# A mixture of experts in blocks of 32 tokens on four column quarters of TensorE, instead of blocks of 64 on two halves

## The chip, the cores and the metric

The kernel runs on one core of one Trainium2 chip. The metric is the device time of one execution in microseconds; lower is better. Median before: 3705.31 us over three runs (3697.03 to 3705.87).

## The reference, cut to what matters

Two transformer blocks over 512 positions of width 1024. The first has a token mixer and then a mixture of experts; the second has attention branches and gates. Only the mixture is touched:

```python
logits = h @ w_router + b_router              # 512 tokens, 32 experts
top_val, top_idx = lax.top_k(logits, 4)
gates = softmax(top_val)
# for each chosen (token, expert) pair:
u = xb @ w1[e] + b1[e]                        # 1024 -> 2048
glu = minimum(u[:, 0::2], 7.0)
lin = clip(u[:, 1::2], -7.0, 7.0)
act = glu * sigmoid(1.702 * glu) * (lin + 1.0)
y = act @ w2[e] + b2[e]                       # 1024 -> 1024
out[token] += gate * y
```

All data are fp32. There are 2048 pairs, and the weights of the 32 experts are 32 x 12 MB.

## The kernel before, in words

`program` runs a sequence of stages, one after the other, with a barrier between them. Three matter here.

`settle` (L1386) ends with the routing. VectorE takes the four best of each token and a rank of each pair within its expert. It counts the blocks of each expert by comparing its token count with `edges`, multiples of 64 (L1553 to L1556); `nblki` holds the counts, `first` the first block of each. L1568 to L1575 build two tables, `who` (token number at its place in a block) and `where` (block of each pair), and 16 matmuls (L1477) make of them `list`, the tokens of each block. `edges`, `halves` and `eye32` are constant tables. SP starts the first 9 weight pieces (EARLY) in this stage. `combine` (L1805), after the experts, gathers the written rows and weighs them.

`experts` (L1593) is the stage in between. Its weights come in pieces of 1 MB, 12 for an expert: eight of the first layer, four of the second. `piece_source` (L1583) says what a piece is: two row groups of 128 and 1024 columns. They lie in a ring of 20 places, `raw`. SP waits for the semaphore `used` in `reload`, piece by piece, and starts the transfer of the piece that is 20 further (L1621). An expert's pieces are released in its last block, since every block of the expert needs them.

Work runs in blocks of up to 64 tokens of one expert. Each engine has its own loop over experts and, inside, over the blocks of the expert, whose number it reads from `nblki` at run time. TensorE's order in one block is written out by hand: bias of the first column half (`bias(0)`, L1685, which picks the expert's bias with the table `pick`), pieces 0 to 3, bias of the second, pieces 4 to 6, the turning of the first activations (`turn_act(0)`, L1704), piece 7, pieces 8 and 9, `turn_act(1)`, the turning of the gathered rows of the next block (`turn_rows`, L1672 and L1674), pieces 10 and 11. A piece is four matmuls (L1698), 128 rows by 64 tokens against 512 columns: for each of two row groups one on each half of the array's columns, so that two run side by side. The two banks `WIDE` hold the first layer, `OUT` the second.

The other engines serve this. VectorE clips the two parts of the first layer (L1791, L1792), multiplies (L1795) and multiplies with ScalarE's sigmoid (L1798). ScalarE makes the sigmoid (L1759), copies the turned activations (L1765) and the turned rows (L1748), copies the result out of `OUT` (L1774) and starts two writes of it to `rows_out` (L1744). POOL makes the index of the next block's tokens (L1649), starts the gather of its rows (L1643) and makes `pick` (L1652). The semaphores between them count blocks (or two per block).

One other place is of use for the prediction: `rwkv_output` computes a part of the modulation at L1149 with four column quarters, 128 rows by 32 columns against 512 columns each.

Of the kernel before, what the change touches and what calls it, by code (L numbers as in the profile page):

```python
# [11 lines left out]
F32 = mybir.dt.float32  # L12
# [7 lines left out]
P = 128  # L20
# [13 lines left out]
E = 32  # L34
# [23 lines left out]
MAXB = 64  # L58

def constants():
# [11 lines left out]
        "edges": np.broadcast_to(64.0 * np.arange(1, 9)[None, :], (P, 8)),  # L73
        "token": P * np.arange(TT)[None, :] + p,
        "headrow": (p % 32) == np.arange(8)[None, :],
        "halves": (p // 64) == (f // 64),
# [1309 lines left out]
def settle(nc, A, ps, T, R, M, N, spill, rows_in, raw_in, stored, kmt):  # L1386
# [6 lines left out]
    with stage(nc, "b_in", "var_ready", "root_ready", "scaled", "normed", "taken", "h_ready", "kept", "saved", "turned", "ht_out", "high", "pool_step",  # L1393
# [6 lines left out]
        def _(sp):  # L1400
            sp.dma_start(R["wr"][:, :, :], A["w_router"][0].rearrange("(k p) e -> p k e", p=P)).then_inc(in_, 16)
            sp.dma_start(R["br"][:, :], A["b_router"]).then_inc(in_, 16)
            b1 = A["b1"][0].rearrange("e (p h n) -> h e p n", p=2, h=2)
            for i in range(4):
                sp.dma_start(N["b1r"][E * i:E * i + E, :].rearrange("e (p n) -> e p n", p=2), b1[i // 2]).then_inc(b_in, 16)
# [8 lines left out]
        def _(pool):  # L1414
# [9 lines left out]
            for i in (1, 3):  # L1424
                lo = slice(E * i, E * i + E)
                done(pool.tensor_tensor(M["b12"][lo, :], N["b1r"][lo, :], M["b12"][lo, :].bitcast(F32), ALU.subtract))

        @block.tensor
        def _(pe):
# [46 lines left out]
            for j in range(JK):  # L1476
                last = pe.matmul(ps[0:64, 7, 0:MAXB], R["who"][:, j, :], R["where"][:, j, :], start=(j == 0), stop=(j == JK - 1))  # L1477
# [3 lines left out]
        def _(act):  # L1481
# [17 lines left out]
            act.activation(M["b12"][:, :], N["b1r"][:, :], ACT.Copy).then_inc(high, 1)  # L1499
# [10 lines left out]
        def _(dve):  # L1510
# [55 lines left out]
            done(dve.scalar_tensor_tensor(out=R["row"][:, :], in0=R["blk"][:, :], scalar=64.0, in1=R["rank"][:, :], op0=ALU.mult, op1=ALU.add))  # L1566
            done(dve.tensor_copy(T["slot"][:, :], R["row"][:, :]))
            done(dve.tensor_tensor(R["over"][:, 0:JK, :], bc(R["rank"][:, :], 2, 8), bc(S("edges"), 1, JK), ALU.is_ge))  # L1568
            done(dve.tensor_reduce(R["low"][:, :], R["over"][:, 0:JK, :], AX_X, ALU.add))
            done(dve.tensor_tensor(R["blk"][:, :], R["blk"][:, :], R["low"][:, :], ALU.add))  # L1570
            done(dve.scalar_tensor_tensor(out=R["low"][:, :], in0=R["low"][:, :], scalar=-64.0, in1=R["rank"][:, :], op0=ALU.mult, op1=ALU.add))
            done(dve.tensor_tensor(R["who"][:, :, :], bc(S("iota")[:, 0:64], 1, JK), bc(R["low"][:, :], 2, 64), ALU.is_equal))
            who = R["who"][:, :, :].rearrange("p (t k) s -> p t (k s)", k=TOPK)
            done(dve.tensor_tensor(who, who, bc(S("token"), 2, TOPK * 64), ALU.mult))
            dve.tensor_tensor(R["where"][:, :, :], bc(S("iota")[:, 0:MAXB], 1, JK), bc(R["blk"][:, :], 2, MAXB), ALU.is_equal).then_inc(listed, 1)  # L1575
            dve.wait_ge(list_prod, 1)
            done(dve.tensor_copy(R["list"][:, :], ps[0:64, 7, 0:MAXB]))

def piece_source(A, e, s):  # L1580

    w1 = A["w1"][0, e].rearrange("(k p) n -> p k n", p=P)
    w2 = A["w2"][0, e].rearrange("(k p) n -> p k n", p=P)  # L1583
    if s < 8:
        return w1[:, 2 * (s % 4):2 * (s % 4) + 2, (s // 4) * D:(s // 4 + 1) * D]
    return w2[:, 2 * (s - 8):2 * (s - 8) + 2, :]

def experts(nc, A, ps, T, R, M, raw_in, stored, cleared, gathered, rows_in, rows_out):
# [3 lines left out]
    HT = 64  # L1593
    TURNED, ROWS_T = 5, 3
    WIDE = (0, 1)
    OUT = 2
    with stage(nc, "used", "indexed", "picked", "bias_done", "turned", "x_out", "biased", "mixed", "sig", "acted", "at", "at_out",
               "y_out", "written") as (
            block, used, indexed, picked, bias_done, turned, x_out, biased, mixed, sig, acted, at, at_out, y_out, written):

        def counter(eng, name, first=0):

            r = eng.alloc_register(name)
            eng.reg_mov(r, first)
            return r, lambda top=MAXB - 1: eng.snap(r, min_val=first, max_val=top)
# [55 lines left out]
        def _(pe):  # L1661
# [1398 lines left out]
```

## Time and profile before

| | |
|---|---|
| median of three runs | 3705.31 us |
| span of the profiled execution | 3706.0 us (no separate time of it is given; its span stands for it) |
| PE busy | 3295.0 us, 89% |
| PE weight loads | 2108.3 us, 57% |
| DVE, ACT, POOL busy | 1399.2, 984.3, 154.3 us |
| DMA | 647.39 MB, mean 175 GB/s |
| stretch of the experts, 979 to 2151 us | PE busy 1144.2 of 1172 us, clock 1.00, DMA share 0.93, 357 GB/s |
| stretch before it, 0 to 979 us | PE busy 780.3 us, DMA share 0.34 |
| stretch after it, 2151 to 3706 us | PE busy 1370.6 us, DMA share 0.26 |

### The profile page before, as it was taken

The numbers are of one execution on the slowest core, as the hardware profiler recorded it, in microseconds if no ns is written. First come the engines' busy times: TensorE is split into PE (matmuls) and PEld (weight loads), VectorE is DVE, ScalarE is ACT, GpSimd is POOL, SyncE is SP. The second block draws the span as 40 slices with busy tenths as digits, with TensorE's granted clock in tenths as the row PEclk, the third lists the DMA queues.
The fourth block names the chain that finished last, engine by engine and source line by source line (L and its number), as shares of the span: only waits on it lengthen the run. The fifth ranks groups of instructions, "written<-read, shape, count | busy, mean of one in ns | idle before, by whom it ended". The sixth has DMA issues, their size and how long they took to land. (4 is left out here: it accounts for less than half of the span.)

```text
span 3706.0 us, 63217 instructions
## 1 busy us (share of the span) xinstructions
PE 3295.0 (89%) x25517; PEld 2108.3 (57%) x25518; DVE 1399.2 (38%) x2384; ACT 984.3 (27%) x1766; POOL 154.3 (4%) x221
## 2 busy tenths in 40 slices
PE   3998788787799997999999969987899899878998
PEld 2878677676433332333333327865578778655787
DVE  5535545546211111111111146544643365446433
ACT  2333313312111111111111103343532233435321
POOL 0000000000300000000000010000000000000000
PEclk8999889888799999999999989997999999979999
DMA  6621320324789999998986944331033133310331
GB/s 217 237 97 33 98 94 8 98 71 157 298 297 396 366 400 399 396 397 320 397 312 244 385 172 122 99 49 35 1 93 101 45 115 101 47 35 1 94 100 57
DMA packets 273124, 647.39 MB, mean 175 GB/s; under 512 B 36890, under 2 KB 97050, under 8 KB 270978
## 3 DMA queue, kind: packets, MB, share of 16 engines
q1 hardware_dynamic: 251314, 605.12, 45.6%
q0 software_dynamic: 6224, 21.24, 1.8%
q10 hardware_dynamic: 15360, 17.82, 1.5%
q8 instruction: 167, 2.74, 0.3%
q14 instruction: 59, 0.48, 0.0%
HBM read 600.85 MB, written 43.27 MB: 174 GB/s over the span
## 5 line engine op out<-in xcount | busy, mean ns | idle before, releaser
L1698 PE MATMUL ps<-raw,ex_xT 128*64 128x512 f32 x3072 | 698.0, 599 | 21.8 <-DMA raw<-in_w_dram 21.7
L1698 PEld LDWEIGHTS ps<-raw,ex_xT 128*64 128x64 f32 x3072 | 206.6, 137 | 419.2 <-issue 375.9
L1791 DVE TENSOR_SCALAR ex_gl<-ps 128x256 f32<-128x256 f32 x96 | 40.8, 425 | 1014.4 <-PE ps L1698 1014.4
L1698 PE MATMUL ps<-raw,ex_aT 128*64 128x512 f32 x1536 | 350.8, 596 | 6.1 <-DMA raw<-in_w_dram 5.5
L1698 PEld LDWEIGHTS ps<-raw,ex_aT 128*64 128x64 f32 x1536 | 105.3, 137 | 205.0 <-issue 187.5
L1950 PE MATMUL ps<-zhi,hh 128*128 128x512 f32 (+1 forms) x448 | 169.8, 379 | 0.4 <-DVE hl L2080 0.4
L1951 PE MATMUL ps<-zlo,hh 128*128 128x512 f32 (+1 forms) x448 | 169.0, 377 | 0.0
L1952 PE MATMUL ps<-zhi,hl 128*128 128x512 f32 (+1 forms) x448 | 168.6, 376 | 0.0
L2497 PE MATMUL ps<-uu_hi,hh 128*128 128x512 f32 x384 | 151.9, 395 | 12.2 <-DVE uu_lo L2609 12.2
L2499 PE MATMUL ps<-uu_hi,hl 128*128 128x512 f32 x384 | 152.2, 396 | 0.0
L2498 PE MATMUL ps<-uu_lo,hh 128*128 128x512 f32 x384 | 152.0, 396 | 0.0
L2609 DVE TENSOR_TENSOR uu_lo<-u_raw,uu_hi 128x2048 fp32r<-128x2048 f32 x30 | 68.6, 2292 | 202.7 <-ACT uu_hi L2575 202.7
L1765 ACT ACTIVATE ex_aT<-ps 128x256 f32<-128x256 f32 x96 | 36.8, 383 | 406.4 <-PE ps L1704 406.4
L2497 PE MATMUL ps<-uu_hi,u_oh 128*128 128x512 f32 x320 | 126.7, 396 | 0.4 <-DVE u_ol L2614 0.4
L2071 DVE TENSOR_TENSOR zlo<-oT,zhi 128x1024 fp32r<-128x1024 f32 (+1 forms) x64 | 74.6, 1166 | 137.2 <-ACT zhi L1987 136.5
L2498 PE MATMUL ps<-uu_lo,u_oh 128*128 128x512 f32 x320 | 126.3, 395 | 0.0
L2499 PE MATMUL ps<-uu_hi,u_ol 128*128 128x512 f32 x320 | 126.3, 395 | 0.0
L1987 ACT ACTIVATE zhi<-oT 128x1024 fp32r<-128x1024 f32 (+1 forms) x64 | 64.9, 1014 | 215.5 <-PE ps L1952 155.6
L1759 ACT ACTIVATE ex_arow<-ex_gl 128x256 f32<-128x256 f32 x96 | 40.0, 417 | 300.1 <-DVE ex_gl L1791 300.1
L2575 ACT ACTIVATE uu_hi<-u_raw 128x2048 fp32r<-128x2048 f32 x30 | 57.3, 1915 | 213.2 <-PE ps L2499 207.2
L2307 ACT ACTIVATE za<-ps,nsa_nm 128x256 f32<-128x256 f32 (+3 forms) x160 | 81.1, 511 | 109.0 <-DVE nsa_nm L2331 109.0
L2270 PE MATMUL ps<-small,za 128*128 128x128 f32 x544 | 86.1, 291 | 16.2 <-DVE za L2342 16.2
(558 smaller groups left out, 6018.8 us busy)
## 6 DMA issues: line engine op xcount, KB each, us to landing
raw<-in_w_dram SPq DMA_DIRECT2D x384, 1024.0 KB, 19.3
oT<-in_w_in_dram SPq DMA_DIRECT2D x64, 512.0 KB, 3.6
u_raw<-in_w_in_dram SPq DMA_DIRECT2D x24, 1024.0 KB, 5.2
expert_out<-xn SPq DMA_DIRECT2D x4, 4096.0 KB, 16.8
expert_out<-ex_yrow ACTq DMA_DIRECT2D x98, 128.0 KB, 6.4
late_ada<-in_w_ada_dram SPq DMA_DIRECT2D x12, 1024.0 KB
early_w<-in_w_in_dram SPq DMA_DIRECT2D x10, 1024.0 KB, 6.6
mT<-in_w_ada_dram SPq DMA_DIRECT2D x4, 2048.0 KB, 19.9
```

The costliest lines, as they stand in the source:

```text
L1698: mm = pe.matmul(o, x, M["raw"][:, (slot + LATE_SLOTS) % RING, k, h * 512:(h + 1) * 512], start=(s >= 8 and kk == 0), stop=(kk == 7))
L1950: pe.matmul(o, x_hi, w_hi, start=(kk == 0), stop=False)
L1951: pe.matmul(o, x_hi, w_lo, start=False, stop=False)
L1952: last = pe.matmul(o, x_lo, w_hi, start=False, stop=(kk == KD - 1))
L1987: act.activation(hi[q % nh][cut], raw[q % nr][cut], ACT.Copy).then_inc(hi_done, 1)
L2071: dve.tensor_tensor(lo[q % nh][cut], raw[q % nr][cut], hi[q % nh][cut].bitcast(F32), ALU.subtract).then_inc(lo_done, 1)
L2270: mm = pe.transpose(ps[:, 4 + x, b * P:(b + 1) * P], Z["p"][:, i % NB, x, b * P:(b + 1) * P], S("ident"))
L2307: act.activation(Z["p"][:, i % NB, x, 0:u["n"]], ps[:, (i % 2) * 2 + x, 0:u["n"]], ACT.Exp, bias=Z["nm"][:, i % 4, x:x + 1], accum_out=Z[" ...
L2497: pe.matmul(o, x_hi, w_hi, start=first, stop=False)
L2498: pe.matmul(o, x_hi, w_lo, start=False, stop=False)
L2499: return pe.matmul(o, x_lo, w_hi, start=False, stop=last)
L2609: dve.tensor_tensor(lo[q % nh], raw[q % nr], hi[q % nh].bitcast(F32), ALU.subtract).then_inc(lo_done, 1)
```

## The change

Blocks hold 32 tokens (HT) and every expert has at least two of them, so each of its first and later blocks can be written out in the code. One matmul is 128 rows by 32 tokens against 512 columns, on a quarter of the array's columns; four stand side by side. In the first layer the quarters are the four column groups of the 2048, so it needs one bank in place of two, and the bias is one pair of matmuls over the whole bank (a high and a low part). In the second layer they are two halves of the 1024 rows of the sum by two column groups; the halves are added afterwards. A piece of the first layer is now one row group with all 2048 columns; a piece of the second is one row group of each half.

TensorE's order per block w: bias and first layer of w, turning of the activations of w-1, turning of the rows of w+1, second layer of w-1. Places of the first layer are released by `used1` in the expert's last block, those of the second by `used2`, in the first block of the next expert. ScalarE copies the upper half of the result (64 partitions), VectorE adds it to the lower, ScalarE starts the writes. ScalarE's loop body begins with the copy of the turned activations, then the turned rows, the sigmoid of the next block and the result.

For the given inputs the experts get these numbers of tokens (counted from the reference): 44, 173, 113, 53, 8, 58, 162, 39, 48, 26, 50, 21, 51, 17, 79, 21, 70, 52, 73, 42, 159, 35, 36, 87, 96, 69, 135, 57, 66, 55, 46, 7. In blocks of 64 that makes 1 or 2 or 3 blocks each, 48 in all; in blocks of 32, with at least two, 87: 2, 6, 4, 2, 2, 2, 6, then seven of 2, then 3, 2, 3, 2, 3, 2, 5, 2, 2, 3, 3, 3, 5, 2, 3, 2, 2, 2.

The diff, cut to its core:

```diff
-MAXB = 64
+MAXB = 128
+HT = 32
+EDGES = SEQ // HT
...
-                last = pe.matmul(ps[0:64, 7, 0:MAXB], R["who"][:, j, :], R["where"][:, j, :], start=(j == 0), stop=(j == JK - 1))
+                last = pe.matmul(ps[0:HT, 7, 0:MAXB], R["who"][:, j, :], R["where"][:, j, :], start=(j == 0), stop=(j == JK - 1))
...
-            done(dve.tensor_tensor(R["over"][:, :, :], bc(cnt, 2, 8), bc(S("edges"), 1, E), ALU.is_gt))
+            done(dve.tensor_tensor(R["over"][:, :, :], bc(cnt, 2, EDGES), bc(S("edges"), 1, E), ALU.is_gt))
             done(dve.tensor_reduce(R["nblk"][:, :], R["over"][:, :, :], AX_X, ALU.add))
+            done(dve.tensor_scalar(R["nblk"][:, :], R["nblk"][:, :], 1.0, None, ALU.max))
+            done(dve.tensor_copy(R["nblki"][:, 0, :], R["nblk"][:, :]))
             done(dve.tensor_scalar(R["nblk"][:, :], R["nblk"][:, :], 1.0, None, ALU.add))
-            done(dve.tensor_copy(R["nblki"][:, :], R["nblk"][:, :]))
+            done(dve.tensor_copy(R["nblki"][:, 1, :], R["nblk"][:, :]))
             done(dve.tensor_tensor_scan(R["first"][:, :], S("ones")[:, 0:E], R["nblk"][:, :], 0.0, ALU.mult, ALU.add))
...
 def piece_source(A, e, s):
 
-    w1 = A["w1"][0, e].rearrange("(k p) n -> p k n", p=P)
-    w2 = A["w2"][0, e].rearrange("(k p) n -> p k n", p=P)
     if s < 8:
-        return w1[:, 2 * (s % 4):2 * (s % 4) + 2, (s // 4) * D:(s // 4 + 1) * D]
-    return w2[:, 2 * (s - 8):2 * (s - 8) + 2, :]
+        return A["w1"][0, e].rearrange("(k p) (a n) -> p k a n", p=P, a=2)[:, s, :, :]
+    return A["w2"][0, e].rearrange("(h k p) n -> p k h n", p=P, h=2)[:, s - 8, :, :]
 
 
...
+                    if s < W1P:
+                        sp.wait_ge(used1, w * W1P + s + 1)
+                    else:
+                        sp.wait_ge(used2, w * W2P + s - W1P + 1)
+                    sp.dma_start(M["raw"][:, place(slot), :, :], piece_source(A, e + ahead // NP, ahead % NP)).then_inc(raw_in[slot], 16)
...
+            def bias(w):
+                pe.wait_ge(picked, w + 1)
+                pe.matmul(ps[:, WIDE, :], M["pick"][:, :], M["b12"][:, 0, :], start=True, stop=False)
+                pe.matmul(ps[:, WIDE, :], M["pick"][:, :], M["b12"][:, 1, :], start=False, stop=False).then_inc(bias_done, 1)
+            def landed(i, place_in_turns):
+                pe.wait_ge(raw_in[place_in_turns % NS], i * (16 * EU * NP // NS) + (16 * (place_in_turns // NS) + 16))
+            def first_layer(w, i, g, fresh):
+                pe.wait_ge(x_out, w + 1)
+                for s in range(W1P):
+                    if fresh:
+                        landed(i, g + s)
+                    for j in range(4):
+                        mm = pe.matmul(ps[HT * j:HT * j + HT, WIDE, :], M["xT"][:, s, :], M["raw"][:, place((g + s) % NS), j // 2, (j % 2) * 512:(j % 2) * 512 + 512],
+                                       start=False, stop=(s == W1P - 1))
+                    mm.then_inc(used1, 1)
+            def turn_act(w):
+                pe.wait_ge(acted, w + 1)
+                for i2 in range(2):
+                    mm = pe.transpose(ps[:, ROWS_T, i2 * P:(i2 + 1) * P], M["arow"][:, i2 * P:(i2 + 1) * P], S("ident"))
+                mm.then_inc(at, 1)
+            def second_layer(w, i, g, fresh):
+                pe.wait_ge(y_out, w + 1)
+                pe.wait_ge(at_out, w + 1)
+                for s in range(W2P):
+                    if fresh:
+                        landed(i, g + W1P + s)
+                    for half in range(2):
+                        for n in range(2):
+                            o = ps[HT * (2 * half + n):HT * (2 * half + n) + HT, OUT, :]
+                            mm = pe.matmul(o, M["aT"][:, 4 * half + s, :], M["raw"][:, place((g + W1P + s) % NS), half, n * 512:(n + 1) * 512],
+                                           start=(s == 0), stop=(s == W2P - 1))
+                    mm.then_inc(used2, 1)
+            def one_block(i, g, before, fresh):
+                w = now()
+                pe.wait_ge(emptied, w)
+                bias(w)
+                first_layer(w, i, g, fresh)
+                turn_act(w - 1)
+                turn_rows(w + 1)
+                second_layer(w - 1, i, before, before == g)
+                pe.reg_add(r, r, 1)
+            def expert(i, e, g):
+                one_block(i, g, g - NP, True)
+                with pe.Fori(0, later_blocks_of(pe, e)) as _:
+                    one_block(i, g, g, False)
 
             turn_rows(0)
-            with pe.Fori(0, E // EU) as i:
+            bias(0)
+            first_layer(0, 0, 0, True)
+            turn_rows(1)
+            pe.reg_add(r, r, 1)
+            with pe.Fori(0, later_blocks_of(pe, 0)) as _:
+                one_block(0, 0, 0, False)
+            whole = (E - 1) // EU
+            with pe.Fori(0, whole) as i:
                 for j in range(EU):
-                    expert(i, j)
-            for j in range(E % EU):
-                expert(E // EU, j)
+                    expert(i, i * EU + (j + 1), NP * (j + 1))
+            for e in range(1 + whole * EU, E):
+                expert(0, e, NP * e)
+            w = now(MAXB)
+            turn_act(w - 1)
+            second_layer(w - 1, 0, NP * (E - 1), False)
...
+            def act_out(w):
+                act.wait_ge(at, w + 1)
+                src = ps[:, ROWS_T, 0:2 * P].rearrange("p (i j s) -> p i j s", i=2, j=4)
+                act.activation(M["aT"][:, :, :].rearrange("p (j i) s -> p i j s", i=2), src, ACT.Copy).then_inc(at_out, 1)
+            def rows_back(w):
+                act.wait_ge(used2, w * W2P + W2P)
+                act.wait_ge(y_out, w + 1)
+                act.activation(M["yhalf"][:, :], ps[2 * HT:4 * HT, OUT, :], ACT.Copy).then_inc(y_half, 1)
+                act.wait_ge(y_out, w + 2)
+                write(w * HT)
+            def body():
+                w = now()
+                act_out(w)
+                rows_turned(w + 2)
+                sigmoid(w + 1)
+                rows_back(w)
+                act.reg_add(r, r, 1)
...
+            def halves_added(w):
+                dve.wait_ge(y_half, w + 1)
+                dve.wait_ge(written, w * 32 + 32)
+                dve.tensor_tensor(M["yrow"][:, :], ps[0:2 * HT, OUT, :], M["yhalf"][:, :], ALU.add).then_inc(y_out, 1)
+            def body():
+                w = now()
+                dve.wait_ge(acted, w + 1)
+                swiglu(w + 1)
+                halves_added(w)
+                dve.reg_add(r, r, 1)
...
```

## Rows read from the trace of the kernel before

**Rows 1.** source view of the expert matmuls' line on PE, first and last start

```profile
L1698 PE MATMUL ps<-raw,ex_xT x3072: 592/592/1114, 979.6 to 2142.2; 128*64 128x512 f32 x192
...
L1698 PE MATMUL ps<-raw,ex_aT x1536: 592/592/644, 995.6 to 2150.4; 128*64 128x512 f32 x192
```

**Rows 2.** stages: PE, PEld, DVE, ACT, POOL busy, PEclk, DMA share, GB/s

```profile
1400.00:1500.00 100.00, 82.62 (x356) 24.17 (x354) 11.37 (x28) 12.65 (x22) 4.95 (x10) 0.98 1.03 399
```

**Rows 3.** waits of SP's queue, expert stage: total us, times, longest

```profile
SPq L1621 <- PE ps L1698: 397.6, 147, 48.2
```

**Rows 4.** timeline of PE over one block: start, us, instruction

```profile
1702.43 0.50 PE L1685 MATMUL ps<-ex_b,ex_pick 128*128 128x512 f32 x1
1702.86 7.09 PE L1698 MATMUL ps<-raw,ex_xT 128*64 128x512 f32 x32
1709.88 0.51 PE L1685 MATMUL ps<-ex_b,ex_pick 128*128 128x512 f32 x1
...
1721.29 0.44 PE L1704 MATMUL ps<-small,ex_arow 128*128 128x128 f32 x2
1721.65 0.43 PE L1672 MATMUL ps<-small,ex_xrow 64*128 64x64 f32 x2
...
1722.45 3.65 PE L1698 MATMUL ps<-raw,ex_aT 128*64 128x512 f32 x16
1726.04 0.50 PE L1685 MATMUL ps<-ex_b,ex_pick 128*128 128x512 f32 x1
```

**Rows 5.** timeline of PE where the transfers bind, turned rows

```profile
1452.09 0.43 PE L1672 MATMUL ps<-small,ex_xrow 64*128 64x64 f32 x2
...
1485.24 0.43 PE L1672 MATMUL ps<-small,ex_xrow 64*128 64x64 f32 x2
```

**Rows 6.** DMA view of the expert stage, gather (q0) and writes (q10)

```profile
q0 software_dynamic: 3840, 12.59, 3.9%
q10 hardware_dynamic: 7680, 12.59, 3.2%
```

**Rows 7.** timeline of PE weight loads: halves (two rows), then quarters

```profile
1703.34 0.14 PEld L1698 LDWEIGHTS ps<-raw,ex_xT 128*64 128x64 f32 x2 [0.28 <-issue]
1703.77 0.14 PEld L1698 LDWEIGHTS ps<-raw,ex_xT 128*64 128x64 f32 x2 [0.29 <-issue]
...
412.29 0.16 PEld L1149 LDWEIGHTS ps<-late_ada,cpad 128*32 128x32 f32 x8 [0.33 <-issue]
412.75 0.13 PEld L1149 LDWEIGHTS ps<-late_ada,cpad 128*32 128x32 f32 x4 [0.30 <-issue]
...
415.87 0.30 PEld L1153 LDWEIGHTS ps<-out_part,mixing 128*128 128x128 f32 x2 [0.84 <-issue]
```

**Rows 8.** DMA view of 1440 to 1460 us, then of 286 to 288

```profile
DMA packets 2087, 8.01 MB, mean 400 GB/s; under 512 B 132, under 2 KB 132, under 8 KB 2087
...
q1 hardware_dynamic: 2014, 7.75, 98.2%
...
DMA packets 98, 0.80 MB, mean 401 GB/s; under 512 B 0, under 2 KB 0, under 8 KB 0
...
q1 hardware_dynamic: 98, 0.80, 96.7%
```

**Rows 9.** timeline of ACT in a block

```profile
1704.78 1.28 ACT L1759 ACT_TABLE_LOAD   x1 [1.64 <-issue]
...
1721.76 0.38 ACT L1765 ACTIVATE ex_aT<-ps 128x256 f32<-128x256 f32 x1 [2.91 <-PE ps L1704]
```

**Rows 10.** gather: POOL's timeline in a block, then time to landing

```profile
1723.66 0.94 POOL L1643 DMA_INDIRECT ex_xrow<-expert_in,ex_index  x1 [0.77 <-POOL ex_index L1649]
...
DMA to landing us min/median/max: 3.6/6.9/8.1
```

**Rows 11.** timeline of the routing, DVE and PE

```profile
962.48 1.23 DVE L1575 TENSOR_TENSOR rt_where<-small,rt_blk 128x1024 f32<-128x1024 f32 x1
...
963.76 3.67 PE L1477 MATMUL ps<-rt_where,rt_who 128*64 128x64 f32 x32 [9.26 <-DVE rt_where L1575]
```

More of the change, by code:

```diff
@@ L72, in constants @@
         "causal": np.where(f <= p, 0.0, NEG),
-        "edges": np.broadcast_to(64.0 * np.arange(1, 9)[None, :], (P, 8)),
+        "edges": np.broadcast_to(float(HT) * np.arange(1, EDGES + 1)[None, :], (P, EDGES)),
         "token": P * np.arange(TT)[None, :] + p,
         "headrow": (p % 32) == np.arange(8)[None, :],
-        "halves": (p // 64) == (f // 64),
+        "quarters": (p // 32) == (f // 32),
         "eye32": (p % E) == np.arange(E)[None, :],
@@ L1592, in experts, with counter, later_blocks_of, every_block_but_one @@
     NP, NS, EU = 12, RING, RING // int(np.gcd(RING, 12))
[L1593 to L1601, printed above, removed]
+    W1P, W2P = 8, 4
+    TURNED, ROWS_T, WIDE, OUT = 5, 3, 0, 2
+    with stage(nc, "used1", "used2", "indexed", "picked", "bias_done", "turned", "x_out", "biased", "emptied", "mixed", "sig", "acted", "at", "at_out",
+               "y_half", "y_out", "written") as (
+            block, used1, used2, indexed, picked, bias_done, turned, x_out, biased, emptied, mixed, sig, acted, at, at_out, y_half, y_out, written):
+        def counter(eng, name):
             r = eng.alloc_register(name)
-            eng.reg_mov(r, first)
-            return r, lambda top=MAXB - 1: eng.snap(r, min_val=first, max_val=top)
+            eng.reg_mov(r, 0)
+            return r, lambda top=MAXB - 1: eng.snap(r, min_val=0, max_val=top)
         def blocks_of(eng, e):
-            return eng.value_load(R["nblki"][0:1, bass.ds(e, 1)], min_val=1, max_val=SEQ // HT)
+            return eng.value_load(R["nblki"][0:1, 1, bass.ds(e, 1)], min_val=2, max_val=EDGES)
+        def later_blocks_of(eng, e):
+            return eng.value_load(R["nblki"][0:1, 0, bass.ds(e, 1)], min_val=1, max_val=EDGES - 1)
+        def every_block_but_one(eng, body):
+            with eng.Fori(0, later_blocks_of(eng, 0)) as _:
+                body()
+            with eng.Fori(1, E) as e:
+                with eng.Fori(0, blocks_of(eng, e)) as _:
+                    body()
+        def place(slot):
+            return (slot + LATE_SLOTS) % RING
         @block.sync
@@ L1662, in _ @@
             r, now = counter(pe, "pe_blocks")
-            pe.sem_inc(used, NP)
             pe.sem_inc(turned, 1)
@@ L1805, in combine @@
+            halves_added(now())
 def combine(nc, A, ps, T, x, G, spill, rows, rows_out, mods):
@@ L2858, in program @@
                                      "sel": [P, TT, E], "gates": [P, TT, E], "eq": [P, TT * TOPK, E], "part": [P, TT * TOPK, E],
-                                     "where": [P, TT * TOPK, MAXB], "first": [P, E], "row": [P, TT * TOPK], "rank": [P, TT * TOPK], "blk": [P, TT * TOPK], "low": [P, TT * TOPK], "over": [P, E, 8], "nblk": [P, E],
-                                     "who": [P, TT * TOPK, 64]}.items():
+                                     "where": [P, TT * TOPK, MAXB], "first": [P, E], "row": [P, TT * TOPK], "rank": [P, TT * TOPK], "blk": [P, TT * TOPK], "low": [P, TT * TOPK], "over": [P, E, EDGES], "nblk": [P, E],
+                                     "who": [P, TT * TOPK, HT]}.items():
                         R[n] = sb(s, "rt_" + n, shape)
```

160 lines of the change are left out of this document (46 added, 114 removed).

## The prediction, made before the change was run

> **What bounds the kernel now.** I read the table of stages first. The expert stage runs from the first weight matmul at 979.6 us to the end of the last at 2151.0 us [rows 1] (last start 2150.4 us, 0.59 us long): 1171.4 us of a span of 3706.0 us. No other stage is rewritten; routing changes a little. In most of it TensorE is full, in 1400 to 1500 us it is 83% busy with the DMA engines full at 399 GB/s, where no record marks 17 of the 100 us [rows 2]. On the other side the queue that loads the weights waited for TensorE in 147 places, 397.6 us in total [rows 3]. So two limits take turns: TensorE where an expert has many blocks, the transfers where experts of one block follow each other.
>
> The timeline gives the block: a bias matmul at 1702.43 us, the next block's at 1726.04 us, so **23.61 us** [rows 4]. 48 blocks make 1133.3 us; the remaining 38.1 us of the 1171.4 are waits for weights. The DMA limit is read where blocks came slower: rows turned at 1452.09 and 1485.24 us, **33.15 us** for an expert of one block [rows 5]. Gather and writes had 3.9% and 3.2% of the DMA engines over 1175 us [rows 6], 1.7 us per block; the other 31.5 us are twelve pieces of weights.
>
> **The change, part by part.** *Number of blocks.* The token counts of the inputs (in the section on the change) give 48 blocks of 64, which the trace has, and 87 of 32, six of them empty fillings from the rule of at least two. By experts: 20 with two blocks, 7 with three, one with four, two with five, two with six.
>
> *A block of TensorE.* Old: 24 pairs. New: 8 + 4 quads. Two bias matmuls back to back, 2 x 0.43 = 0.87; first layer 16 slots, 7.03; turning the activations as one step, 0.36 (1721.29 to 1721.65); turning the rows, 0.80 before with 64 columns [rows 4], with 32 between 0.4 (half) and 0.80: nine weight loads of unchanged width stay, so 0.72; second layer 8 slots, 3.59. Sum **12.57 us**; x 87 = 1093.6 us, 39.7 less than before. The gain sits in the seven experts with three blocks (37.7 against 47.2 us); two-block experts lose (25.1 against 23.6).
>
> *The bytes.* Each expert's 12 MB are loaded once, as before. What changes is the shape: a first-layer piece is now rows of 8 KB that lie together in memory and in the ring, before it was 4 KB runs. The loads of today show 4 KB packets (no packet of 8 KB): 7.75 MB at a share of 98.2% of 20 us is 395 GB/s; a stretch with 8 KB packets alone moved 0.80 MB at 96.7% of 2 us, 414 GB/s [rows 8]. So eight of twelve pieces could go 5% faster, a DMA-bound expert in 33.15 - 8/12 x 0.05 x 31.5 = 32.1 us (gather and writes cost half per block, and there are two blocks). Bounds: nothing gained (33.15), or all twelve 5% faster (31.6). I take 32.1, as the form of the access is nearest to the 8 KB row.
>
> The page "DMA: Bandwidth & Descriptors" of the Trainium skill (section on where 436 GB/s comes from) puts HBM to SBUF at some 358 GB/s for one core, by which packet size could gain nothing here. The trace disagrees with the figure, at 399 GB/s.
>
> *The waits for weights.* I kept a running balance over the 384 pieces: a transfer starts when the one before is done and its place is free, and takes 2.68 us (32.1 / 12); TensorE starts a piece once it has landed; a landing is never under 5.5 us after the release. Run with the old kernel's rows (2.76 us, release inside the block) it gives 38 us of waits, against 38.1 measured. For the new one it gives **50.5 us**: more, since a two-block expert needs 25.1 us where its weights need 32.1, and since the second layer's four places are freed one first layer later, so that only 16 of 20 run ahead. It falls (experts counted from 0) in the first block (2.7), expert 6 (6.5), experts 10 to 14 (35: after seven two-block experts in a row the store is gone), the rest near 16 to 20. With 2.76 us per piece it is 69 us, with 2.62 us 38 us.
>
> *Chains that must stay covered.* (a) The second layer waits for ScalarE's copy of the turned activations: 0.47 us after the transposes start, 0.38 long [rows 4, 9], so 0.85 us against the 1.08 us that the turned rows give. Margin 0.2 us, priced at nothing; if it is gone, see the rival. (b) The activation of a block has a whole second layer and next first layer behind it, over 11 us, for two clips, sigmoid (with its table load of 1.28 us) and two products, some 4 us: nothing. (c) One bank for the first layer: the next bias waits for two clips of 0.4 us, behind 4.7 us of other TensorE work: nothing. (d) Gathering: from turned rows 1.2 us from TensorE's end on them (1722.45) to the issue, at most 8.1 us to the landing [rows 10], together 9.3 us of the 11.8 us that a block now leaves. VectorE's step that adds the halves waits for the last write (priced like a gather, 8.1 us at most to land [rows 10]) and for ScalarE's copy; queued behind it is the next clip, 6 us later. Covered, at nothing, with 2.5 us in hand. (e) On the queues of SP and POOL no step is moved past another; SP's reload of second-layer pieces waits longer, which is in the balance.
>
> *Routing.* VectorE takes 1.2 ns per element (1.23 us for 1024) [rows 11]. The compares over edges and their reductions double (+768 elements in four operations, +0.9 us), two small operations of 0.2 us are new, the place table doubles (+1.2), the who table halves, twice (-1.2): +1.3 us. The list matmuls stream 128 instead of 64 columns, 3.67 us before [rows 11], between +0 and +3.7; I take +3.2, as they run with the clock down. All of it stands ahead of the first gather: +4.5 us. The end: after ScalarE's copy comes one addition before the write, +0.8 us.
>
> **Sum**: 1093.6 + 50.5 = 1144.1 against 1171.4: -27.3; +4.5 + 0.8 = **-22 us**. The profiled execution's span is 3706.0 us and the median of the runs 3705.3, with nothing to speak of around the span, so both give **3684 us**.
>
> **Rivals.** *B, the transfers stay as fast as now.* The DMA view cannot show that the new access becomes 8 KB packets. Then 69 us of waits, stage 1162.6 us, total 3702 us: no difference. A measurement of this kernel tells 0.3% (11 us) from no change.
>
> *C, slower: a wait ahead of every second layer.* Place: ScalarE's copy of the turned activations, the first operation of its loop body, where before the sigmoid was. One table load of 1.28 us stands ahead of the sigmoid today and starts before the wait it precedes (1704.78 us, while its input comes from the section that ends at 1709.88) [rows 4, 9], which speaks against. Should a load fall between transposes and copy, it shows 1.28 - 0.2 = 1.05 us per block; 87 x 1.05 = 91 us, less 29 us that the DMA waits give back, -22 + 62 = +40: 3746 us. It decides from 0.6 us per block on, where the time is 0.3% above today's.
>
> *D, slower: four quarters do not keep the slot.* Rows 7 show it for eight slots, and not beside full transfers; here four streams read beside 400 GB/s of writes. Against it: halves keep 0.43 us beside full DMA. At 0.50 us a slot, 24 x 0.07 x 87 = 146 us, less 40 given back, less 22: 3790 us. The Trainium skill ("TensorE: Matmul & The Clock Gate", measured speedup vs the span model) reports 2.38 times for three column tiles, 79% of full; by that rule, as an estimate, the slot would be 0.54 us and the time near 3870 us. The 3.58 us for eight slots of four disagree.
>
> *E, faster: more from the packets.* All pieces 5% faster, 2.62 us each with the side traffic: 38 us of waits, 12 less: 3671 us.
>
> **Numbers.** Forecast A 0.50 (own range 3668 to 3696), B 0.20, C 0.12, D 0.05, E 0.13. Faster by over 0.3% (under 3694): 0.46 of A, all of E, 0.03 of B: 0.62. Within: 0.04 of A, 0.15 of B and 0.01 of C: 0.20. Slower: 0.11 of C, D, and 0.02 of B with longer release times: 0.18. Range: from E's lower part, 3655, up to 3722, where most of C and all of D lie beyond.
>
> **What would show it.** Block period 12.5 to 12.7 us where DMA is below full (five- and six-block experts); 87 rows of the activation copy; weight loads of 32 columns, four per 0.43 us; expert period near 32 us in experts 10 to 13; packets of 8 KB in the weight queue; no wait for ScalarE at TensorE; TensorE's waits for weights up by a third, not down. Wrong would be: a period over 12.9 us (C or D: in D the slots themselves are wider), only 4 KB packets (B), or a routing stage longer by more than 8 us.

## The result, and the profile after

The changed kernel takes 3715.71 us (median of 20 runs, 3702.46 to 3729.99), the kernel before beside it 3705.97 us: a ratio of **1.0027 [1.0017, 1.0037]**, some 10 us slower. Once more on another chip (six runs) it was 1.0041 [1.0027, 1.0055]. The time lies within the predicted range, but the 22 us forecast as a gain did not come, and the small difference has the other sign.

The profiled execution has a span of 3728.2 us and is the slowest of those runs. The first bias matmul of the experts also comes at times between 962 and 984 us in the traces of this case, for reasons in stages that nobody changed. So profiles are compared below by **the stage**: from the first bias matmul to the first matmul of `combine`. It is 1181.3 us before and 1197.4 us after, +16.1 (1194.2 in the second trace of the same kernel, +12.9; of the kernel before there is this one trace).

The view by stretches: length; busy time of PE, PEld, DVE, ACT and POOL with instructions; clock; DMA share; GB/s. First before:

```profile
978.78:2160.12 1181.34, 1144.40 (x5330) 384.16 (x5329) 158.19 (x396) 197.76 (x339) 73.81 (x145) 1.00 0.93 355
```

After, whole stage, then the stretch of [rows 2]:

```profile
984.44:2181.83 1197.39, 1125.32 (x9484) 365.85 (x9484) 201.42 (x447) 148.01 (x352) 130.32 (x262) 0.96 0.89 349
1400.00:1500.00 100.00, 84.45 (x642) 25.62 (x638) 13.73 (x30) 9.98 (x24) 8.87 (x18) 0.88 1.02 404
```

TensorE is busy 19 us less than before, though its clock is 0.96 where it was 1.00, and it stands still for 35 us more (72.1 against 36.9 us that no record covers). In 1400 to 1500 us the DMA engines are full as before, but the clock is down to 0.88.

One block of TensorE after (timeline: start, duration, instruction), which answers to [rows 4]:

```profile
1247.63 0.50 PE L1694 MATMUL ps<-ex_b,ex_pick 128*128 128x512 f32 x1
1247.97 0.39 PE L1695 MATMUL ps<-ex_b,ex_pick 128*128 128x512 f32 x1
1248.29 7.07 PE L1708 MATMUL ps<-raw,ex_xT 128*32 128x512 f32 x64
1255.30 0.44 PE L1716 MATMUL ps<-small,ex_arow 128*128 128x128 f32 x2
1255.66 0.40 PE L1686 MATMUL ps<-small,ex_xrow 32*128 32x32 f32 x2
1255.91 0.60 PE L1688 MATMUL ps<-small,ex_xrow 32*128 32x32 f32 x7
1256.43 3.64 PE L1729 MATMUL ps<-raw,ex_aT 128*32 128x512 f32 x32
1260.00 0.50 PE L1694 MATMUL ps<-ex_b,ex_pick 128*128 128x512 f32 x1
```

12.37 us from bias to bias. And its weight loads, which answer to [rows 7], here with the DMA engines at work:

```profile
1249.60 0.13 PEld L1708 LDWEIGHTS ps<-raw,ex_xT 128*32 128x32 f32 x4 [0.30 <-issue]
1250.03 0.13 PEld L1708 LDWEIGHTS ps<-raw,ex_xT 128*32 128x32 f32 x4 [0.30 <-issue]
```

The waits of the stage (total us, times, longest), after and then before:

```profile
PEld ps L1708 <- DMA raw<-in_w_dram: 74.5, 39, 2.9
...
PE ps L1708 <- DMA raw<-in_w_dram: 39.5, 31, 2.0
...
PE ps L1694 <- issue: 20.0, 5, 4.2
...
PE ps L1729 <- ACT ex_aT L1786: 3.0, 1, 3.0
```

```profile
PEld ps L1698 <- DMA raw<-in_w_dram: 57.6, 44, 2.9
...
PE ps L1698 <- DMA raw<-in_w_dram: 27.2, 40, 2.0
```

PEld's row lies beside matmuls still running; PE's is the part in which nothing runs. There is more waiting for weights than before, and one row is new: five times PE waits for "issue" ahead of an expert's bias, 20.0 us in all. Before, PE has no such row. The 35 us in which TensorE stands longer are these: 20.0 for issue, 12.3 more for weights, and the 3.0 us of the last row.

**Where the stage goes.** With a block of 12.375 us, every block that took longer can be listed; the stage is then a sum (to 0.2 us):

| | after | without transfers (`tiny_after`, below) | forecast |
|---|---|---|---|
| 87 blocks | 1076.6 | 1076.6 | 1093.6 |
| last matmul to `combine` | 9.2 | 9.2 | (as before) 9.1 |
| first blocks of experts 0 and 1, while the ring fills | 8.7 | 8.4 | 2.7 |
| last second layer, late and at low clock | 4.8 | 5.8 | 0 |
| around the five turns of TensorE's loop over experts (last block of experts 5, 10, 15, 20, 25 and first of the next) | 36.0 | 7.3 | waits 47.8 |
| first blocks of experts 5, 9, 10, 12, 13, 14, 20, 23, 31 | 62.2 | 0 | (in the 47.8) |
| sum | 1197.5 | 1107.3 | 1153.2 |

The kernel before has 48 x 23.61 = 1133.3 us, the same 9.1 us, and 38.9 us more. The faster block gave 17 us more than forecast; the two rows ahead of the sum took 50 us more than forecast, and the two above them 11 us more.

A part of these rows is not standing but slow work. In the last first block, shown further down, the granted clock is 0.52 from 2145 to 2151 us, that is 1.2 GHz. From the turned activations to the next bias seven first blocks (experts 1, 9, 12, 13, 14, 20, 31) take 1.7 to 3.5 us more than the 4.70 us of an ordinary block, 17.6 us in all.

### The profile page after: what moved, and what is told of

The parts are those of the page before. It is cut to its first block and busy times, and to the rows that moved or that the text cites. A ratio compares the mean times of both kernels' runs of the same rounds, so it can differ in the third digit from the quotient of the medians.

```text
span 3728.2 us, 72571 instructions
## 1 busy us (share of the span) xinstructions
PE 3283.6 (88%) x29672; PEld 2091.0 (56%) x29673; DVE 1441.9 (39%) x2437; ACT 933.9 (25%) x1779; POOL 206.7 (6%) x337
## 5 line engine op out<-in xcount | busy, mean ns | idle before, releaser
L1708 PE MATMUL ps<-raw,ex_xT 128*32 128x512 f32 x5568 | 641.5, 609 | 39.7 <-DMA raw<-in_w_dram 39.5
L1708 PEld LDWEIGHTS ps<-raw,ex_xT 128*32 128x32 f32 x5568 | 170.2, 111 | 459.9 <-issue 384.4
L1729 PE MATMUL ps<-raw,ex_aT 128*32 128x512 f32 x2784 | 331.2, 618 | 3.0 <-ACT ex_aT L1786 3.0
L1822 DVE TENSOR_SCALAR ex_gl<-ps 128x256 f32<-128x256 f32 x87 | 36.9, 424 | 643.7 <-PE ps L1708 643.7
L1729 PEld LDWEIGHTS ps<-raw,ex_aT 128*32 128x32 f32 x2784 | 84.0, 113 | 175.0 <-issue 171.4
L1834 DVE TENSOR_TENSOR ex_yrow<-ps,ex_yhalf 64x512 f32<-64x512 f32 x87 | 59.4, 683 | 288.3 <-ACT ex_yhalf L1791 288.3
L1791 ACT ACTIVATE ex_yhalf<-ps 64x512 f32<-64x512 f32 x87 | 51.6, 594 | 269.0 <-PE ps L1729 269.0
```

Of the source, the lines that this page charges most:

```text
L1708: mm = pe.matmul(ps[HT * j:HT * j + HT, WIDE, :], M["xT"][:, s, :], M["raw"][:, place((g + s) % NS), j // 2, (j % 2) * 512:(j % 2) * 512 + ...
L1729: mm = pe.matmul(o, M["aT"][:, 4 * half + s, :], M["raw"][:, place((g + W1P + s) % NS), half, n * 512:(n + 1) * 512], start=(s == 0), stop ...
```

## The experiments

`tiny_*` leave out most of the reloads' bytes, so that most matmuls work on the first pieces loaded; all others compute the whole reference. "Stage" is as above; a ratio is against the kernel before on the same chip.

### Without the transfers: tiny_after and tiny_before

```diff
-sp.dma_start(M["raw"][:, place(slot), :, :], piece_source(...))
+sp.dma_start(M["raw"][:, place(slot), 0, 0:64], piece_source(...)[:, 0, 0:64])
```

> Each reload moves 32 KB in place of 1 MB, so the second layer and the first work on stale weights from expert 1 on; what TensorE does is unchanged. Shows the stage without transfers as a limit. Theory 1 (TensorE's own rows: 87 x 12.37 = 1076 us and 5 code stalls of 4 to 7 us, 1100 to 1110 us for the stage against 1188): span 3640 to 3655 us. Theory 2 (chains through the other engines also wait now and then): stage over 1120 us.

> The same cut of the reloads in the old kernel. Expected by its rows: 48 x 23.61 = 1133 us for the stage against 1171, span 3668 us. So with transfers out of the way the changed kernel should lead by 13 to 28 us, where with them it is 10 us behind: then the loss sits in how transfers and work meet. If it does not lead here, the loss is TensorE's own.

Ratios 0.9791 [0.9772, 0.9811] and 0.9909 [0.9889, 0.9930], 3622.28 and 3665.82 us. The stages, changed kernel first:

```profile
970.29:2077.83 1107.54, 1085.95 (x9485) 361.81 (x9484) 201.62 (x447) 148.01 (x352) 130.38 (x262) 0.99 0.16 43
```

```profile
982.12:2125.70 1143.58, 1134.56 (x5330) 386.78 (x5329) 158.12 (x396) 197.76 (x339) 73.70 (x145) 1.00 0.16 43
```

With 32 KB in place of 1 MB per piece the change is worth 36.0 us of stage and 43.5 us of time. That is more than the 13 to 28 us expected, and the span of 3624.9 us lies under the 3640 to 3655 expected. The forecast of TensorE's own work comes near (1093.6 + 9.1 us to `combine` = 1102.7, measured 1107.5), in part by luck: the blocks took 17 us less, and the start, the end and the turns of the loop 21.5 us, for none of which it had a price but the 2.7 us of the first block. The loss against the kernel before lies in what the transfers add: 1181.3 - 1143.6 = **37.7 us** before, 1197.4 - 1107.5 = **89.9 us** after, where the forecast had 38 and 50.5.

### The loop over experts: flat

TensorE's program for five experts (ten blocks, since the first and the later ones are written apart) is a loop body with six turns. `flat` writes all 31 experts out:

```diff
-            whole = (E - 1) // EU
-            with pe.Fori(0, whole) as i:
-                for j in range(EU):
-                    expert(i, i * EU + (j + 1), NP * (j + 1))
-            for e in range(1 + whole * EU, E):
+            for e in range(1, E):
```

> TensorE's loop over groups of five experts is written out, so that its program has no long jump back; nothing else changes. In the trace of the changed kernel TensorE stands 4 us (reason: issue) at the start of experts 6, 11, 16, 21 and 26, and instruction loads run all through the stage, where the old kernel loaded none. Theory 1 (code is fetched anew at each turn of the loop, 5 x 4 us plus 5 blocks at the low clock): those stalls vanish and the time falls by 8 to 25 us against the changed kernel, not the full 36, since waits for weights take a part. Theory 2 (the transfers set the time anyway): stalls vanish, waits for weights grow by the same, time within 4 us. Theory 3 (the stall is the loop register or a semaphore): it stays.

1.0007 [0.9997, 1.0017], stage 1187.6 us: 7 to 10 us less than with the loop (by the two ratios 7 to 13 us of time). What it takes away is this, in the changed kernel's timeline (the first matmul after a turn; in brackets how long PE had stood):

```profile
1219.36 0.79 PE L1694 MATMUL ps<-ex_b,ex_pick 128*128 128x512 f32 x1 [3.95 <-issue]
...
1220.50 1.08 PE L1708 MATMUL ps<-raw,ex_xT 128*32 128x512 f32 x4
```

The DMA view of the stage shows what runs on the queue that brings instructions (packets, MB, share): after, before, then `flat`.

```profile
q8 instruction: 67, 1.10, 0.4%
```

```profile
q8 instruction: 6, 0.10, 0.0%
```

```profile
q8 instruction: 55, 0.90, 0.3%
```

Before, whose loop has half as many block bodies, almost nothing is fetched in this stage. After, TensorE's program comes anew with each turn, and behind full weight queues that costs 4 us of standing; without them (`tiny_after`) the same five cost

```profile
PE ps L1694 <- issue: 6.9, 5, 1.8
```

`flat` fetches nearly as much, but straight ahead, and no wait for issue is left at L1694. The trace also has the times of these packets. Around the turn at 1219.36 us they start at 1216.5, 1222.4 and 1228.4 us, 6 us apart, and much the same at the other four turns; without the transfers they come 3 to 4 us apart (1196.2, 1199.5, 1203.4 us), and in `flat` never closer than 11 us. That the waits go with the loop, and that TensorE stands while code is brought, is shown; that the length of the body is what makes it be fetched again was not tried and rests on the packet counts.

### Only packets of 4 KB: pad4k

The halves of each ring place are set 32 bytes apart, so that no 8 KB row lies together; all else is the changed kernel.

```diff
-M = {"raw": nc.alloc_sbuf_tensor_at("raw", [P, RING, 2, D], ...
+M = {"raw": nc.alloc_sbuf_tensor_at("raw", [P, RING, 2, D + 8], ...
```

> The two halves of each ring place are moved 32 bytes apart, so that a first-layer piece lands as runs of 4 KB as in the old kernel; nothing else changes. Theory 1 (8 KB packets are worth 2.5%, 401 against 391 GB/s for a packet of each size in the two traces): packets of 8 KB vanish, waits for weights grow, time +5 to +14 us. Theory 2 (packet size is worth the 5% of the prediction): +15 to +25 us. Theory 3 (worth nothing, as the memory side limits): within 3 us.

1.0059 [1.0046, 1.0073]; on its chip that is 3721.34 us, 7 to 12 us over the changed kernel by the two ratios of that. The interval overlaps that of the higher ratio. Its profiled execution (3699.28 us) is the lowest of its runs, so its stage of 1190.8 us says little. The DMA view of 1400 to 1500 us: the weight queue before, then the changed kernel, then `pad4k`:

```profile
q1 hardware_dynamic: 9948, 38.32, 97.7%
```

```profile
DMA packets 7715, 40.36 MB, mean 404 GB/s; under 512 B 877, under 2 KB 877, under 8 KB 4525
...
q1 hardware_dynamic: 6843, 38.65, 96.7%
```

```profile
DMA packets 10881, 40.28 MB, mean 403 GB/s; under 512 B 875, under 2 KB 875, under 8 KB 10875
...
q1 hardware_dynamic: 10011, 38.60, 97.7%
```

The first layer does come in 8 KB packets (7715 packets in place of 10881 for the same bytes). 38.65 MB at a share of 96.7% of 100 us is 400 GB/s, 38.60 MB at 97.7% is 395: **1.2% for the mixture, where some 3% were taken** (5% for two thirds of the bytes; by the mean duration of one packet over the stage of the changed kernel, 326.7 ns against twice 167.4, those of 8 KB run 2.5% faster). 400 GB/s is again above the 358 GB/s that the prediction had quoted from the Trainium skill ("DMA: Bandwidth & Descriptors", where 436 GB/s comes from); by that page it is a core's half of what two cores of a pair share, and here one core runs alone.

### The order of the work: flat_mid, loop_mid, flat_spread, mid_late

The first block of a new expert needs eight pieces in 7 us, while one lands every 2.7 us. The move puts the previous block's second layer, which works on places already loaded, between its first-layer pieces:

```diff
                 bias(w)
-                first_layer(w, i, g, fresh)
+                first_layer(w, i, g, fresh, 0, 3)
                 turn_act(w - 1)
+                first_layer(w, i, g, fresh, 3, 4)
+                second_layer(w - 1, i, before, before == g, 0, 3)
+                first_layer(w, i, g, fresh, 4, W1P)
+                second_layer(w - 1, i, before, before == g, 3, W2P)
                 turn_rows(w + 1)
-                second_layer(w - 1, i, before, before == g)
```

`flat_mid` has this on `flat`, and `loop_mid` on the changed kernel with its loop.

> The written-out loop, and the second layer of the block before is done inside the first layer of the block: turned activations after piece 2, three pieces of it after piece 3, the last after piece 7. The places of the second layer are free some 4 us sooner after an expert's last block, and work stands between the waits for new pieces. Theory 1 (late release of the second layer's four places costs, as the prediction's balance had it; with the measured rates the same balance gives 9 us less): time 5 to 20 us under the written-out kernel. Theory 2 (only transfer rate and TensorE's own time count): within 4 us, or slower by the added sections (0.15 us a section, 13 us in all).

> The kernel with the written-out loop and the second layer inside the first, once more, for a comparison on one chip. Expected: 0.995 of the kernel before, 0.9935 to 0.9965.

> The changed kernel with its loop over groups of five experts, and the second layer moved inside the first: the move alone. From the two effects taken as independent (the written-out loop 7 to 13 us, the move 18 us by time, 28 us in the stage): 0.998 of the kernel before, 18 us under the changed kernel. If the code stalls of 4 us are hidden by the transfers once the ring runs better, it comes near 0.996.

| | loop kept | written out |
|---|---|---|
| order of the change | 1.0027 and 1.0041; stage 1197.4, 1194.2 | 1.0007; 1187.6 |
| second layer moved | 0.9982 [0.9968, 0.9995]; 1176.2 | 0.9948 [0.9931, 0.9964] and 0.9930 [0.9913, 0.9947]; 1159.7, 1165.4 |

The move is worth 18 to 28 us of stage, where 5 to 20 us of time had been expected, and the loop 7 to 17 us. Together they beat the changed kernel and the kernel before, with 3682.84 and 3679.82 us, 18 and 23 us under the latter on the same chips.

What the move removes is read in the first block of the last expert, in the changed kernel:

```profile
2127.88 0.39 PE L1695 MATMUL ps<-ex_b,ex_pick 128*128 128x512 f32 x1
2128.20 2.78 PE L1708 MATMUL ps<-raw,ex_xT 128*32 128x512 f32 x24
2131.32 1.07 PE L1708 MATMUL ps<-raw,ex_xT 128*32 128x512 f32 x8 [0.33 <-DMA raw<-in_w_dram]
2133.67 1.06 PE L1708 MATMUL ps<-raw,ex_xT 128*32 128x512 f32 x8 [1.29 <-DMA raw<-in_w_dram]
2136.46 1.06 PE L1708 MATMUL ps<-raw,ex_xT 128*32 128x512 f32 x8 [1.73 <-DMA raw<-in_w_dram]
2138.97 1.06 PE L1708 MATMUL ps<-raw,ex_xT 128*32 128x512 f32 x8 [1.44 <-DMA raw<-in_w_dram]
2141.48 1.93 PE L1708 MATMUL ps<-raw,ex_xT 128*32 128x512 f32 x8 [1.45 <-DMA raw<-in_w_dram]
...
2145.27 6.32 PE L1729 MATMUL ps<-raw,ex_aT 128*32 128x512 f32 x32
2151.52 0.50 PE L1694 MATMUL ps<-ex_b,ex_pick 128*128 128x512 f32 x1
```

Three pieces are there; the other five come one by one every 2.3 to 2.8 us, and the second layer, which could have run between them, comes last and, at the lower clock, takes 6.3 us in place of 3.6. The block takes 23.98 us, and 14.89 with the move. The other first blocks from which the waits went: expert 1 18.06 to 12.61, expert 5 15.72 to 12.76, expert 9 17.27 to 12.77. Experts 10 to 14 keep theirs (15.5 to 21.6 us), where the DMA engines are full, and experts 6, 16 and 20 still take 18.2, 18.8 and 15.6 us.

An ordinary block of `flat_mid`:

```profile
1220.24 2.78 PE L1708 MATMUL ps<-raw,ex_xT 128*32 128x512 f32 x24
1222.95 0.44 PE L1716 MATMUL ps<-small,ex_arow 128*128 128x128 f32 x2
1223.32 1.06 PE L1708 MATMUL ps<-raw,ex_xT 128*32 128x512 f32 x8
1224.20 2.76 PE L1729 MATMUL ps<-raw,ex_aT 128*32 128x512 f32 x24
1226.78 3.62 PE L1708 MATMUL ps<-raw,ex_xT 128*32 128x512 f32 x32
```

Two explanations were open: TensorE has other work while pieces land, or the second layer's places are given back earlier. `mid_late` takes the second away:

```diff
-sp.wait_ge(used2, w * W2P + s - W1P + 1)
+sp.wait_ge(used2, w * W2P + W2P)
```

> The same kernel, but the transfers into the second layer's four places wait for the whole second layer (its last piece stands at the block's end), so that they are released about 11.5 us into the next block, as late as in the written-out kernel without the move (9.4 to 12.1 us), in place of 5.4 to 7.2 us. TensorE's order of work is unchanged. Theory 1 (what the move bought is the earlier release): the gain of 28 us in the stage falls back, stage 1180 to 1190 us, time near 1.000 of the kernel before. Theory 2 (it bought work that stands between the waits for new pieces): stage stays near 1160 us, 0.995.

0.9964 [0.9947, 0.9980], stage 1167.3. Against `flat_mid_again`, on the same chip, some 9 us of time (and 2 to 8 us of stage) are the release; the two intervals just touch. SP's queue waits for these places 276.6 us in `flat`, 134.8 in `flat_mid` and 192.9 in `mid_late`. The remaining 16 us of time (1.0007 to 0.9964, on two chips) are the order of the work. How much of them is the clock, which such work between the waits keeps up, was not tried.

> The second layer's pieces of the block before stand one by one between pieces 3 to 7 of the first layer, in place of three in a row. Theory 2 (work between waits): 2 to 6 us better than three in a row. Theory 1 (release): the releases come 1 to 3 us later, the same or 2 us worse.

`flat_spread` deals the second layer's pieces singly between pieces 4 to 7 of the first: 0.9934 [0.9916, 0.9951], stage 1160.9. That is no different from `flat_mid_again`; the 2 to 6 us expected did not come.

### The clock: flat_warm, and the same kernel again

`flat_warm` puts a matmul of 128 columns by 512 (two records, 1.19 us with what follows) behind each of the first seven pieces, in the first block of the experts where weights were late:

```diff
                     mm.then_inc(used1, 1)
+                    if fresh and s < W1P - 1 and g // NP in (1, 5, 6, 9, 10, 11, 12, 13, 14, 18, 20, 23, 31):
+                        pe.matmul(ps[:, 6, :], S("ident"), T["small"][:, 0:512], start=True, stop=True)
```

> The written-out loop, and in the first block of 13 experts that had to wait for weights (1, 5, 6, 9 to 14, 18, 20, 23, 31) one more matmul of 512 columns, of constants, into a bank of its own after each of the first seven pieces (0.86 us each, while a piece comes every 2.7 us). It keeps TensorE at work between the waits. Theory 1 (waits at a third of the work let the clock fall to 1.2 GHz, and the rest of the block, 3.6 us of second layer, then takes 6.3): mean clock of the stage rises from 0.95 to 0.99, the second layer of those blocks is back at 3.6 us, time 5 to 25 us under the written-out kernel. Theory 2 (the low clock falls where transfers set the time anyway): the clock rises and the time stays within 5 us. Where an expert did not have to wait, the fillings cost 6 us each, up to 20 us in all.

1.0054 [1.0036, 1.0072], stage 1203.1 us. In experts 10 to 14 (timeline of one such block, shortened):

```profile
1434.52 0.50 PE L1694 MATMUL ps<-ex_b,ex_pick 128*128 128x512 f32 x1
...
1435.18 1.06 PE L1708 MATMUL ps<-raw,ex_xT 128*32 128x512 f32 x8
1436.17 1.12 PE L1712 MATMUL ps<-small 128*128 128x512 f32 x2
1437.23 1.07 PE L1708 MATMUL ps<-raw,ex_xT 128*32 128x512 f32 x8
...
1451.67 3.64 PE L1731 MATMUL ps<-raw,ex_aT 128*32 128x512 f32 x32
1455.24 0.50 PE L1694 MATMUL ps<-ex_b,ex_pick 128*128 128x512 f32 x1
```

and its waits for weights:

```profile
PEld ps L1708 <- DMA raw<-in_w_dram: 1.1, 2, 0.8
```

The second layer is back at 3.64 us, hardly anything waits for weights, and **the stretch of experts 10 to 14 is no shorter**. `flat`, then `flat_warm`:

```profile
1357.66:1535.88 178.22, 158.55 (x1203) 47.87 (x1199) 25.19 (x55) 18.34 (x44) 16.33 (x33) 0.88 1.02 403
```

```profile
1368.32:1546.19 177.87, 177.87 (x1273) 52.31 (x1270) 25.18 (x55) 18.31 (x44) 16.34 (x33) 1.00 1.02 403
```

The clock rose from 0.88 to 1.00, and the DMA engines are full at 403 GB/s in both, so the stretch lasts what its transfers last. Each first block is 20.72 us long, 8.35 of them fillers. In this stretch the low clock costs nothing; outside it the fillers cost up to what they last. That it costs something in blocks outside such a stretch, as the last expert's, is argued from their lengths, not shown by a run.

> The changed kernel as it is, for a comparison on one chip with the next two. Expected: 1.0027 of the kernel before, as measured, within its interval of 0.001 (3 to 20 us behind).

`after_again` is the changed kernel unaltered, on the chip of `flat_mid` and `flat_warm`: the ratio told at the top, stage 1194.2. Its waits fall otherwise over the experts (in expert 14 10.8 us, before 6.8) with nearly the same sum, so single blocks of one trace are good to some microseconds, the stage to about 3.

## Why the prediction was wrong, step by step

- **A block of TensorE, 12.57 us**: 12.37. Two biases 0.66 (forecast 0.87: the second follows after 0.34, the first layer after 0.32), first layer 7.01 (7.03), turned activations 0.36 (0.36), turned rows 0.77 (0.72), second layer 3.57 (3.59). Right but for the biases, 17 us over 87 blocks.
- **Four quarters keep the slot (rival D)**: four loads of 32 columns each 0.43 us beside full transfers. D is out. The rule of the Trainium skill ("TensorE: Matmul & The Clock Gate", measured speedup vs the span model), from which 0.54 us a slot had been estimated, does not hold for fp32 with four tiles here.
- **The packets, 5% for eight of twelve pieces**: 8 KB packets came, so rival B's ground falls, but they give 2.5% each. The period of an expert of one old block was 33.15 us; experts 10 to 13 now take 33.2 (32.7 and 32.1 in `after_again` and `flat`) against 32.1 forecast. The direction was right, the size wrong; `pad4k` puts the whole of it at 7 to 12 us of time.
- **Waits for weights, 50.5 us**: this is the step that failed. By the difference with and without transfers they are 89.9 us (before 37.7, forecast 38), and what waits without transfers is not even in that. The forecast put 35 us on experts 10 to 14 and 2.7, 6.5 and about 6 elsewhere; first blocks there have 36.6 us over 12.37 (without the code wait ahead of expert 11), but the others, forecast next to nothing, cost too: expert 5 3.4, 9 4.9, 20 8.3, 23 2.2, 31 11.6. Three things are shown to be in it:
  - the loop's turns: 20 us of standing for code, a cost for which the prediction had no term at all. Transfers go on meanwhile, so its removal gives 7 to 10 us with this order;
  - transfers slower than forecast: the weight queue moved 0.9% more in 100 us (38.65 against 38.32 MB) where the forecast had 3%. By the prediction's balance, 18.5 us of waits for 0.08 us a piece, that is some 13 us, an estimate;
  - the order of the work. The balance let TensorE wait piece by piece, but took the second layer as given at the end, and the price of that place never stood in the sum. `flat_mid` shows it: 22 to 28 us of stage, with the earlier release.

  These sizes overlap, since an early wait fills the store for a later one. The low clock behind the waits, 17.6 us in seven blocks, had no term either; `flat_warm` shows that it costs nothing in experts 10 to 14, and no run shows its price outside them. Even with the measured rate, the code waits and the clock put in, the balance falls short of the stage by an estimated 10 us or more, and that part stays open.
- **Chain (a), the copy of the activations, margin 0.2 us, and rival C**: no wait for ScalarE in 86 blocks; one of 3.0 us at the very end, outside the loops. There the last copy stands in ScalarE's order behind the issue of the writes of the block before (2165.60 us, 0.81 long), which in the loops a whole first layer hides:

```profile
2166.80 0.38 ACT L1786 ACTIVATE ex_aT<-ps 128x256 f32<-128x256 f32 x1 [2.18 <-issue]
```

  With the low clock behind it, it costs 4.8 us that were counted at 0. The table loads of the sigmoid went from 48 to one, which the prediction had not seen:

```profile
L1781 ACT ACT_TABLE_LOAD x1 | 1.3, 1283 | 0.0
```

- **Where the gain sits**: the prediction named the seven experts with three blocks. The two with five gain too, by its own figures 8 us each (62.9 against 70.8), and those with four and six lose; its sum over all blocks has them right.
- **Chains (b) to (e)** at nothing: right. PE waits for VectorE once, 0.2 us, and its weight loads twice for ScalarE's copy of the rows, 1.0 us in all.
- **SP's reload of second-layer pieces waits longer, in the balance**: `mid_late` measured it, some 9 us of time.
- **Routing, +4.5 us**: from the first routing matmul on the chosen experts to the first bias 28.75 us before, 30.6 after, 30.5 to 32.5 in the other traces of the new routing: +1.9 to +3.7. Its two terms were of the right kind, the list matmuls +2.1 (forecast +3.2) and the place table +1.06 (+1.2), by these rows, which answer to [rows 11]. The end, forecast at +0.8, is +0.1 (9.16 against 9.09 us from the last matmul to `combine`).

```profile
966.43 2.29 DVE L1576 TENSOR_TENSOR rt_where<-small,rt_blk 128x2048 f32<-128x2048 f32 x1
...
968.77 5.79 PE L1476 MATMUL ps<-rt_where,rt_who 128*32 128x128 f32 x32 [10.49 <-DVE rt_where L1576]
```

- **The chances**: 0.27% over the kernel before lies within 0.3%, which had 0.20, three quarters of it for B; the 0.41% of the second measurement lies beyond, which had 0.18. That the time fell into the range at all is luck: the sum behind it was some 40 us short in the stage. B named the transfers' rate, and that is a part of it; most of the loss came from when the pieces are wanted, not from how fast they come. No rival named the order of the work or the loop's code.

## What to carry to other kernels

A kernel that alternates between two limits gains from a faster engine only where that engine binds: here the blocks gained more than forecast, and the waits took it back. So draw up demand against supply inside a block, not only over an expert: if the first block of a new expert wants eight pieces in a third of the time in which they land, put work whose data is there between them. And count how much code a loop's body has once first and later turns are written apart; standing at each turn of the loop shows as a wait for issue ahead of its first instruction, with packets on the instruction queue.

## What the runs showed of the hardware that was not expected

- TensorE stood 3.95 us at a turn of a loop whose body had doubled, with 67 instruction packets in the stage against 6, and at most 1.8 us when the weight queues were nearly idle.
- The two bias matmuls over one bank of 512 columns, one record each with the same weights, take 0.34 and 0.32 us to the next start, not a slot of 0.43 as the single one before did [rows 4].
- After some microseconds of piecewise waiting the same 32 records of the second layer take 5.0 to 6.3 us in place of 3.6; keeping the clock up by fillers (1.00 against 0.88) gained nothing in a stretch with the DMA engines full.
- ScalarE loaded a table 48 times in the stage before and once after. What else stands between the sigmoids is the same kind of copy as before, so the changed order of the loop body is the likely reason; it was not tried.
